# Two blocks on one core: 64 tokens instead of 48 through gathered rows, two buffers for u rows, one set of one-hot buffers

## What is computed

```python
def peer(h, w_q, sub_k1, sub_k2, exp_u, exp_v):
    ...
    expert = e1 * PEER_NKEYS + e2          # [256 tokens, 8 heads, 16]
    gate = jax.nn.softmax(sv, axis=-1)
    ...
        u = exp_u[ec]
        a = jax.nn.gelu(jnp.einsum('cd,chkd->chk', xc, u).astype(jnp.float32))
        w = (gc * a).astype(exp_v.dtype)
        return jnp.einsum('chk,chkd->cd', w, exp_v[ec])
```

## Time and profile before

| | before |
|---|---|
| median of 3 runs | 3191.44 us (3190.96 to 3194.03) |
| span of the profiled execution | 3200.7 us |
| TensorE busy | 3146.6 us, 98% |
| VectorE busy | 2275.1 us, 71% |
| ScalarE busy | 1258.0 us, 39% |
| expert layer, units 0 to 127 | 693 to 1903 us |
| data moved by DMA | 821.53 MB |

### The profile page before, as it was taken

The page is one execution under the profiler, slowest core; times in us unless marked ns, Lnnn a source line. Parts: engine busy times, 40 slices in busy tenths (PEclk is TensorE's granted clock), DMA queues, the critical chain, the costliest instruction groups (busy, mean ns, idle before and its releaser), DMA issues.

```text
span 3200.7 us, 71241 instructions
## 1 busy us (share of the span) xinstructions
PE 3146.6 (98%) x31196; PEld 2824.5 (88%) x31196; DVE 2275.1 (71%) x2708; ACT 1258.0 (39%) x1132; POOL 349.6 (11%) x290
## 2 busy tenths in 40 slices
PE   7999999999999999999999999999999999999998
PEld 4877778899999999999999988888888888888887
DVE  8596276799998877777798784688477766655554
ACT  2000143445544444444444444444443444433332
POOL 0276100000011122121222000300000000000000
PEclk9999989999999999999999999999999999999999
DMA  9658685556788999999899866556565566566663
GB/s 409 273 216 356 272 359 216 194 177 231 240 296 320 369 319 357 343 352 347 328 344 340 291 215 207 200 197 200 168 223 199 185 198 205 199 199 202 203 198 118
DMA packets 105299, 821.53 MB, mean 257 GB/s; under 512 B 12394, under 2 KB 14458, under 8 KB 15552
## 3 DMA queue, kind: packets, MB, share of 16 engines
q1 hardware_dynamic: 84960, 683.71, 59.7%
q0 software_dynamic: 17520, 128.11, 10.5%
q10 hardware_dynamic: 2592, 6.29, 0.5%
HBM read 814.00 MB, written 4.06 MB: 256 GB/s over the span
## 4 chain that ended last, share of the span: by engine, by line
PE 85%; DVE 10%; DMA 2%; issue 1%; ACT 1%; DVEq 0%; SPq 0%; ACTq 0%; POOLq 0%
PE psW L608 22%; PE psW L610 22%; PE psW L609 22%; PE psW L606 7%; DVE ring L1300 4%; DMA ring<-wst_dram 2%; PE psM L681 1%; PE psW L781 1%; PE psM L953 1%; PE psM L669 1%; PE psM L610 1%; PE psM L608 1%; PE psM L609 1%; PE psM L781 1%; PE psM L734 1%
## 5 line engine op out<-in xcount | busy, mean ns | idle before, releaser
L1300 DVE SCALAR_TENSOR_TENSOR ring<-ring 128x2048 f16<-128x2048 f32 x526 | 1201.8, 2293 | 572.5 <-ACT ring L2193 570.4
L2193 ACT ACTIVATE ring<-ring 128x2048 f16<-128x2048 f32 x526 | 1002.5, 1907 | 925.0 <-PE psW L610 825.9
L608 PE MATMUL psW<-h_act,ring 128*128 128x256 f16 (+1 forms) x5008 | 1326.2, 265 | 7.7 <-DVE ring L1300 4.7
L609 PE MATMUL psW<-h_act,ring 128*128 128x256 f16 (+1 forms) x5008 | 1325.7, 265 | 0.0
L610 PE MATMUL psW<-h_act,ring 128*128 128x256 f16 (+1 forms) x5008 | 1325.6, 265 | 0.0
L608 PE MATMUL psW<-arena,ring 128*128 128x208 f16 (+1 forms) x3072 | 796.7, 259 | 0.9 <-DVE arena L1887 0.9
L610 PE MATMUL psW<-arena,ring 128*128 128x208 f16 (+1 forms) x3072 | 796.4, 259 | 0.0
L609 PE MATMUL psW<-arena,ring 128*128 128x208 f16 (+1 forms) x3072 | 796.4, 259 | 0.0
L608 PEld LDWEIGHTS psW<-h_act,ring 128*128 128x128 f16 x5008 | 490.4, 98 | 64.8 <-issue 13.9
L610 PEld LDWEIGHTS psW<-h_act,ring 128*128 128x128 f16 x5008 | 490.6, 98 | 33.9
L609 PEld LDWEIGHTS psW<-h_act,ring 128*128 128x128 f16 x5008 | 490.6, 98 | 33.6
(11 more groups left out here) (437 smaller groups left out, 2578.9 us busy)
## 6 DMA issues: line engine op xcount, KB each, us to landing
ring<-wst_dram SPq DMA_DIRECT2D x522, 1024.0 KB, 5.4
ring<-wst_dram SPq DMA_DIRECT2D x64, 2048.0 KB, 11.1
arena<-wst_dram POOLq DMA_DIRECT2D x6, 2048.0 KB, 13.4
proj<-h_rows POOLq DMA_DIRECT2D x6, 1024.0 KB
x_res<-xT_dram POOLq DMA_DIRECT2D x2, 2048.0 KB, 14.0
arena<-wst_dram ACTq DMA_DIRECT2D x2, 2048.0 KB, 14.8
out_dram<-x_res SPq DMA_DIRECT2D x4, 512.0 KB, 2.9
bias_rows<-proj POOLq DMA_DIRECT2D x1, 1536.0 KB, 12.5
```

The costliest lines, as they stand in the source:

```text
L608: nc.tensor.matmul(out, whi(s, col, P), xh, start=first, stop=False)
L609: nc.tensor.matmul(out, whi(s, col, P), xl, start=False, stop=False)
L1300: ins = stt(wlo(s, c, n), ring[:, s * UNIT + c:s * UNIT + c + n], WSCALE, whi(s, c, n), ALU.mult, ALU.subtract)
L2193: act(whi(s, p2 * (UNIT // 2), UNIT // 2), ring[:, c], ACT.Copy, scale=WSCALE).then_inc(hi_done, 1)
```

## The change

64 tokens go by rows and 192 the dense way. So there are 12 steps of 16 tokens in place of 13, and 64 u rows, 64 v rows and 8 `h_load` in place of 48, 48 and 6; the rows are added to the result in two batches of 32 in place of 24. The tables of slots are stretched over the same units: a dot every 1.33 units (2.1 after a group) in place of 1.85 (2.8), a product every 1.4 in place of 1.85. The u rows get a second buffer, in the space that the smaller activations leave free. `hot2` and `hot1` lose theirs, and VectorE makes the operands of step k+1 after gating step k. The lists of rows are four in place of three, and their place against `turn_picks` is changed.

```diff
-ROWS_T = 48
+ROWS_T = 64
-BATCH_T = 24
+BATCH_T = 32
...
-        at += 2.8 if i % HEADS == HEADS - 1 else 1.85
+        at += 2.1 if i % HEADS == HEADS - 1 else 1.33
...
-        at = max(at + (1.85 if i < ROWS_T - GROUP_T else 1.25), GELU_AT[i // HEADS] + 2)
+        at = max(at + (1.4 if i < ROWS_T - GROUP_T else 1.25), GELU_AT[i // HEADS] + 2)
...
+U_BUFS = 2
-    u = [(DOT_HALF[i - 1] / 2 + 1.7 if i else 0.0, "u", i) for i in range(ROWS_T)]
+    u = [(DOT_HALF[i - U_BUFS] / 2 + 1.7 if i >= U_BUFS else 0.1 * i, "u", i) for i in range(ROWS_T)]
...
-        row_buf = [A[:, 14336:16384], J[:, 0:2048], J[:, 4096:6144]]
+        row_buf = [A[:, 14336:16384], A[:, 12288:14336], J[:, 0:2048], J[:, 4096:6144]]
...
-        hot2 = [buf.bitcast(F16).rearrange("p (t e x) -> p t e x", t=STEP_T // 2, x=2) for buf in (A[:, 13312:14336], J[:, 6144:7168])]
+        hot2 = J[:, 6144:7168].bitcast(F16).rearrange("p (t e x) -> p t e x", t=STEP_T // 2, x=2)
...
                 if qb:
                     pe_.wait_ge(pickT_sb, 1)
                     pe_.wait_ge(gate16_ready, 1)
+                else:
+                    pe_.wait_ge(list_taken, 1)
...
+                if u == 10:
+                    for b in range(4):
+                        row_lists(b)
                 for qb in range(2):
-                    if u == 10 + 8 * qb:
+                    if u == 12 + 6 * qb:
                         turn_picks(qb)
-                if u == 10:
-                    for b in range(3):
-                        row_lists(b)
...
-                for j in range(3):
+                for j in range(4):
                     ins = v.tensor_reduce(tok_diag[:, j, :], ident[:, :].rearrange("p (a k) -> p a k", k=TOPK), AX_X, ALU.add)
...
-                v.wait_ge(hot_used, STEPS * q + n + 1)
+                v.wait_ge(hot_used, STEPS * q + n + 2)
...
-                if 11 <= u < 14:
+                if 11 <= u < 15:
                     take_list(u - 11)
...
-                if u == 17:
-                    hot(0, 1)
                 for _, k in steps:
                     gated(0, k)
-                    hot(0, k + 2)
+                    hot(0, k + 1)
                     gated_low(0, k)
...
+                if kind == "h":
+                    if i:
+                        g.wait_ge(dot_done, HEADS * i)
+                    h_load(i)
+                    continue
                 if kind == "u":
-                    if i:
-                        g.wait_ge(dot_done, i)
-                    if i % HEADS == 0:
-                        h_load(i // HEADS)
+                    if i >= U_BUFS:
+                        g.wait_ge(dot_done, i - U_BUFS + 1)
```

More of the change, by code:

```diff
@@ L256, in slots @@
     return [i for i, at in enumerate(table) if at == 16 * ORDER.index(name) + n]
-ROW_BUFS = 3
+ROW_BUFS = 4
+U_BUFS = 2
 V_BUFS = 2
 def row_loads():
-    u = [(DOT_HALF[i - 1] / 2 + 1.7 if i else 0.0, "u", i) for i in range(ROWS_T)]
+    u = [(DOT_HALF[i - U_BUFS] / 2 + 1.7 if i >= U_BUFS else 0.1 * i, "u", i) for i in range(ROWS_T)]
     v = [(PRODUCT_AT[i - V_BUFS] + 1.2 if i >= V_BUFS else PRODUCT_AT[i] - 3.0, "v", i) for i in range(ROWS_T)]
-    return [load[1:] for load in sorted(u + v)]
+    h = [(DOT_HALF[HEADS * g - 1] / 2 + 1.7 if g else 0.0, "h", g) for g in range(ROWS_T // GROUP_T)]
+    return [load[1:] for load in sorted(u + v + h)]
 ROW_LOADS = row_loads()
-ROW_PLACE = {("u", i): (0, 16 * (i + 1)) for i in range(ROWS_T)}
-ROW_PLACE.update({("v", i): (1 + i % V_BUFS, 16 * (i // V_BUFS + 1)) for i in range(ROWS_T)})
+ROW_PLACE = {("u", i): (i % U_BUFS, 16 * (i // U_BUFS + 1)) for i in range(ROWS_T)}
+ROW_PLACE.update({("v", i): (U_BUFS + i % V_BUFS, 16 * (i // V_BUFS + 1)) for i in range(ROWS_T)})
 class Chain:
@@ L390, in program @@
         ident16 = dyn[:, 384:448].bitcast(F16)
-        tok = dyn[:, 0:72].rearrange("p (j t) -> p j t", t=BATCH_T)
-        tok_diag = dyn[:, 0:96].rearrange("p (j x) -> p j x", x=BATCH_T + GROUP_T)[:, :, 0:GROUP_T]
+        tok = dyn[:, 0:128].rearrange("p (j t) -> p j t", t=BATCH_T)
+        tok_diag = dyn[:, 0:160].rearrange("p (j x) -> p j x", x=BATCH_T + GROUP_T)[:, :, 0:GROUP_T]
         slot16 = dyn[:, 160:176]
         row_pick = J[:, 2048:2176]
[L395 to L398, removed]
+        row_val = rs[:, 0:128].rearrange("p (g f h) -> p g f h", f=2, h=HEADS)
+        dots = rs[:, 128:192].rearrange("p (g h) -> p g h", h=HEADS)
+        row_index = rs[:, 192:256].bitcast(U32)
+        row_of = J[:, 6144:7168]
         row_part = A[:, 14336:14848]
-        row_bank = [psM[:, 0, :], psM[:, 1, :], psM[:, 3, :]]
+        row_bank = [psM[:, 2, :], psM[:, 0, :], psM[:, 1, :], psM[:, 3, :]]
         row_w = H[:, :].rearrange("p (c x) -> p c x", x=P)[:, :, 0:BATCH_T]
@@ L440, in program @@
         iota16 = dyn[:, 256:384].bitcast(F16).rearrange("p (e x) -> p e x", x=2)
-        hot2 = [buf.bitcast(F16).rearrange("p (t e x) -> p t e x", t=STEP_T // 2, x=2) for buf in (A[:, 13312:14336], J[:, 6144:7168])]
+        hot2 = J[:, 6144:7168].bitcast(F16).rearrange("p (t e x) -> p t e x", t=STEP_T // 2, x=2)
         first1 = W[:, 1536:1792].bitcast(F16).rearrange("p (t e x) -> p t e x", t=STEP_T // 2, x=2)
-        hot1 = [buf.bitcast(F16).rearrange("p (t r e x) -> p t r e x", t=STEP_T // 2, r=2, x=2)
-                for buf in (W[:, 1024:1536], dyn[:, 448:960])]
+        hot1 = W[:, 1024:1536].bitcast(F16).rearrange("p (t r e x) -> p t r e x", t=STEP_T // 2, r=2, x=2)
         def routed(b):
@@ L668, in route @@
                     for r in range(2):
-                        mm = nc.tensor.matmul(psM[:, b, t * QUART_T:(t + 1) * QUART_T], hot2[b][:, t // 2, :, t % 2],
-                                              hot1[b][:, t // 2, r, :, t % 2],
+                        mm = nc.tensor.matmul(psM[:, b, t * QUART_T:(t + 1) * QUART_T], hot2[:, t // 2, :, t % 2],
+                                              hot1[:, t // 2, r, :, t % 2],
                                               start=(r == 0), stop=(r == 1))
@@ L1797, in take_list @@
                 tmp = row_part.rearrange("p (x k) -> p x k", k=TOPK)
-                step(tt(tmp, row_bank[b].rearrange("p (x k) -> p x k", k=TOPK), slot16.unsqueeze(1).to_broadcast([P, 32, TOPK]),
-                        ALU.mult))
+                tt(tmp, row_bank[b].rearrange("p (x k) -> p x k", k=TOPK), slot16.unsqueeze(1).to_broadcast([P, 32, TOPK]),
+                   ALU.mult).then_inc(list_taken, 1)
+                v.wait_ge(list_taken, b + 1)
                 step(v.tensor_reduce(rs[:, 32 * b:32 * b + 32], tmp, AX_X, ALU.add))
-                if b == 2:
+                if b == 3:
+                    D.wait()
                     v.tensor_copy(row_index.rearrange("p (g h) -> p g h", h=HEADS), row_val[:, :, 0, :]).then_inc(index_ready, 1)
@@ L1869, in hot @@
                 tt(first1, numbers(QUART_T * q, QUART_T), by_pairs(e16[:, 0, :], QUART_T), ALU.is_equal).then_inc(first1_ready, 1)
-                tt(hot2[b], numbers(0, P), by_pairs(e16[:, 1, :], P), ALU.is_equal).then_inc(hot2_ready, 1)
+                tt(hot2, numbers(0, P), by_pairs(e16[:, 1, :], P), ALU.is_equal).then_inc(hot2_ready, 1)
                 v.wait_ge(first1_ready, STEPS * q + n + 1)
                 for r in range(2):
-                    ins = tt(hot1[b][:, :, r, :, :], first1, by_pairs(g16[:, r, :], QUART_T), ALU.mult)
+                    ins = tt(hot1[:, :, r, :, :], first1, by_pairs(g16[:, r, :], QUART_T), ALU.mult)
                 ins.then_inc(hot1_ready, 1)
@@ L1944, in _ @@
                         gated(r, k)
-                        hot(r, k + 2)
+                        hot(r, k + 1)
                         gated_low(r, k)
@@ L2477, in _ @@
                     c = u - 5
-                    a.wait_ge(masks_ready, 5)
+                    a.wait_ge(masks_ready, 6)
                     a.wait_ge(h_row_ps, c + 1)
```

14 lines of the change are left out of this document (7 added, 7 removed).

## The result

The changed kernel took 3211.02 us (median of 4 runs, 3209.48 to 3215.74) beside 3192.74 for the kernel before on the same chip (4 runs, 3190.96 to 3194.34): a ratio of 1.0051 [1.0039, 1.0063]. It is 0.5% slower; 0.4% faster was predicted, and 3211 lies above the range.

What follows compares the result with a forecast made beforehand. TensorE bounds the kernel before; after the change DMA was to bound units 32 to 110. A gain of 49.4 us less 36 lost to transfers left 13.4: 3191.4 - 13.4 = 3178 us, 0.4% faster, range 3150 to 3208.

Steps and rivals of the forecast that it cites:

- sum without transfers: Units 0 to 127: about 3 us gained by unit 31 plus 46.4 after it, 49.4 us if transfers keep up.
- end of unit 31: Units 18 to 31: TensorE gains 8.4 us net, waits for single operands take 5.5, leaving about 3 us.
- units 32 to 127: Smaller matmuls save 61.4 us, 16 more row products cost 17.4, three fewer routed steps give 2.4: 46.4 us gained.
- one steady pace: Units 32 to 110: DMA sets 9.55 us a unit, 39 us over TensorE's need, less 3 for lead: 36 lost.
- The clock: Waits inside a unit can cost TensorE granted clock; nothing was counted, as it has time to spare while awaiting transfers.
- The idle time: TensorE's waiting in units 32 to 110 behind late transfers, put at 36 us, with bounds of 30 and 77.
- price of the `h_load`: Each token vector load slows the queues for 18 us to about 265 GB/s, costing 8.9 us of transfer time.
- The transfers keep up: Rival: full queues hide the waits in units 32 to 110, so nearly all 49.4 us stand; 3142 us, chance 0.15.
- The efficiency of now: Rival: engines keep 382 GB/s at full share, 10.07 us a unit in units 32 to 110; 3219 us, chance 0.22.
- One set of operands: Rival: operands behind late halves stop TensorE in units 96 to 108, adding 5 to 15 us; 3183 to 3193, chance 0.12.
- HBM grants no more than 347: Rival: 347 GB/s is all the core gets, 10.55 us a unit in units 32 to 110; 3257 us, chance 0.02.
- What would show it: Signs: TensorE waiting some 35 us for halves in units 32 to 110, DMA at 385 to 400 GB/s, `v0` 3 us earlier.

Runs made afterwards that it cites:

- four copies: The fifth experiment: the changed kernel with each token vector written to HBM 4 times, each copy read 4 times per `h_load`; 3143.93 us, ratio 0.9828 to the kernel before.
- first: The changed kernel with each token vector written to HBM 16 times, so an `h_load` reads no row twice; 3150.72 us, ratio 0.9854 to the kernel before.
- second: The changed kernel with token vectors loaded for the first group only, leaving the rows part of the result wrong; 3148.74 us, ratio 0.9858 to the kernel before.
- tenth experiment: The changed kernel with each `h_load` reading its 8 rows in 16 rounds, not each 16 times running, result wrong; 3167.49 us, 0.9926 of the kernel before.
- sixth: The changed kernel with each token vector written to HBM 2 times, each copy read 8 times per `h_load`; 3170.83 us, ratio 0.9911 to the kernel before.

## Why the prediction was wrong

**What held.** The sum without transfers was 49.4 us. With four copies, where the transfers do keep up, the stages together take 1160.3 us, 49.4 less than before. By part:

| part | predicted | with four copies |
|---|---|---|
| end of unit 17 | 1.7 later | 1.4 later |
| end of unit 31 | 3 earlier | 4.0 earlier |
| units 32 to 127 | 46.4 gained | 45.4 gained |

That the sums agree to a tenth is luck, since the parts are 1 us off in opposite directions. The terms hold: units take 7.92 us bare, 8.72 with a routed step and 9.02 with a product, and the weights set no floor that shows at 192 columns.

**What failed: units 32 to 110 were given one steady pace, that of the transfers.** The prediction took 9.55 us for each of the 79 units, "the queues will be full", took 3 us off for the lead, and had 36 us lost. It put nothing for transfers in units 18 to 31. TensorE lost 59.8 us in units 32 to 110 ((629.0 + 147.4) - (576.1 + 140.5)), 9.83 us a unit, and 7.1 in units 18 to 31 (133.4 - 126.3). That is the whole miss: 23.8 + 7.1 = 30.9 of the 31.0 us between -13.4 and +17.6.

There was no steady pace. Of the 79 units 61 take the same time as with four copies, within 0.1 us: TensorE's own. The 59.8 us stand in the other 18, behind the seven loads, but for some 3 us in units 97 to 99. Between two loads TensorE can't make good what it lost. Two terms were wrong by that:

- *The clock, "I count nothing".* TensorE's busy time for the same matmuls is 14.4 us longer than with four copies (589.15 + 141.41 against 575.63 + 140.50), as its granted clock is 0.97 in units 32 to 95 and not 1.00. The prediction let this pass since TensorE had time to spare. It has none once it is at its own pace again, and half-speed matmuls are lost there.
- *The idle time.* It is 45.4 us more than with four copies, where 36 were predicted: 9.4 too few.

In units 18 to 31 it is the same: behind the first load, halves come late, the operands behind them too, and TensorE waits 5.8 us at one routed step.

The price of the `h_load`, 8.9 us, was not the step that failed. Windows of 24 us from the issue of a load, one of the kernel before, one of the changed kernel, and the 12 us that follow on this:

```profile
1607.60:1631.60 24.00, 24.00 (x319) 24.00 (x317) 19.98 (x24) 9.41 (x8) 2.44 (x2) 1.00 0.99 292
...
1313.30:1337.30 24.00, 24.00 (x333) 23.13 (x332) 12.73 (x14) 8.26 (x6) 2.01 (x3) 1.00 1.02 300
1337.30:1349.30 12.00, 7.37 (x70) 6.86 (x68) 8.08 (x6) 3.82 (x2) 4.65 (x2) 0.78 0.72 248
```

| after a load, GB/s | loads from the second on | mean |
|---|---|---|
| before, first 24 us | 290, 272, 307, 287, 292 | 290 |
| changed, first 24 us | 265, 277, 273, 300, 295, 299, 324 | 290 |
| changed, next 12 us | 335, 347, 355, 248, 341, 412, 404 | 349 |

The slow stretches are no deeper than before. By the prediction's way of reckoning, 24 us at 290 GB/s are 6.96 MB, 5.91 of them not the load's own, which take 14.4 us at 411: a load costs 9.6 us, 0.7 more than it said. But in the 12 us behind that the DMA engines have a share of only 0.72 to 0.88 after four of the seven loads. There the queues aren't full; the dots are late, and GpSimd asks for rows only after them. How the 9.4 us fall to these two is not shown.

**What lay behind.** The prediction took the slow load as given and asked only what it costs. The first, second and fifth experiments show that the load as it is written costs the stages 67.0 us (1227.3 - 1160.3), though it needs only 64 KB of different data, and that its megabyte isn't what costs. Of the 52.9 us in units 32 to 95, 13.8 go when 16 reads in rounds become one (tenth experiment), and the step from 8 reads to 4 is worth 17.7 (sixth): so much is the repeated reads. The rest hangs on the form with 8 rows read 16 times in a run, and whether the runs make it or the other packets is open. One edit outside the change turns the changed kernel from 0.5% slower into 1.7% faster.

**The rivals.** *The transfers keep up* was wrong of this kernel and right of the one with copies: 3142 was its time, 3143.93 is measured there. *The efficiency of now* gave 3219 and the right sign; by its own condition (49.4 + 3 over TensorE's 715.5) it decides from 9.72 us a unit, not 9.68, and 9.83 passes both. But its mechanism, 382 GB/s between loads, is refuted: the 376 GB/s over 550 us are a mean of some 399 between loads (1228 to 1312, 407 at full share) and of stretches at 246, and with four copies 406 is held throughout. *One set of operands* has its loop (before, 5.8 + 4.2 us), and what the rival foresaw is there in small: in units 96 to 110 of the changed kernel TensorE waits three times for the operands, 5.1 us in all, the low end of its 5 to 15. It needs the late transfers for that: with four copies, still on one set, the same units hold 140.50 us of TensorE busy in 140.50. *HBM grants no more than 347* is refuted by 406 over 550 us.

**What would show it.** TensorE does wait for halves behind ScalarE's waits for `wst_dram`, but 15.0 us and not some 35; most of its idleness, 24.8 us, is for v rows, which the prediction didn't name. `v0` starts 301.5 us after unit 0 (168.1 + 133.4), 3.2 later than before (166.7 + 131.6), where 3 earlier was predicted, and the rate is not 385 to 400 but 372, at a share of 0.98.

## What to carry to other kernels

A load that reads few rows many times can slow every queue of the core well past its own bytes, and while an engine has a lead no time shows it; look at GB/s beside the busy share in the stretch behind it before you raise the demand. When such stretches come every few units, don't spread their cost over a mean pace: an engine that goes at its own pace between them can't catch up, so go through one period, with the lead, the requests that stand behind late work in a queue, and the clock that TensorE loses after each wait. Before pricing a slow stretch, ask whether it has to be there: four copies in HBM cost nothing and were worth 67 us.

## What the runs showed of the hardware

- A load of 1 MB from 8 rows of 8 KB, each read 16 times in a run, brought all DMA traffic of the core to 246 to 247 GB/s over 15 us, with the engines busy throughout (share 1.03). 8 reads gave 309, of which the first 8 us were at 244; 4 reads gave 421. 16 reads in rounds over the rows gave 313. Why is open. That fewer reads of a row cost less is shown from 8 to 4, and the two forms with 16 reads show that their number isn't all; the one in runs of 16 also has 128 more packets. That it is one part of HBM that is asked too often is only a guess. The Trainium skill (DMA: Bandwidth & Descriptors, Latency and other measured facts) tells of HBM copies at 207 GB/s with a row pitch of 512 KiB, 164 at 2 MiB and 103 at 4 MiB, and infers channel aliasing; no run here varies the pitch, so none tests it.
- Gathers and weight loads together held 406 GB/s at a share of 0.99 for 550 us, and 421 for 15. The Trainium skill (HBM Reference, Specifications (TRN2)) gives about 425 for a core that streams alone, which these runs agree with.
- Writing 8 MB from SBUF to HBM took 47.1 us beside the loads of weights, and in the changed kernel stretched units 12 and 13 to 15.25 and 10.4 us, where four copies leave them 8.25 and 7.92; 2 MB landed in 13.9 us and cost nothing that the stages show.
